# Differential attention with scores and maxima issued ahead of turns and combination, outputs one unit later

## What is computed

```python
def diff_attn_core(q, k, v, lam):
    s = jnp.einsum('bqhmd,bkhmd->bhmqk', q, k).astype(F32) * (B_HEAD_DIM ** -0.5)
    p = jax.nn.softmax(s, axis=-1)
    a = p[:, :, 0] - lam * p[:, :, 1]
    return jnp.einsum('bhqk,bkhd->bqhd', a.astype(v.dtype), v)
```

## Time and profile before

| | us |
|---|---|
| median of 3 runs | 1687.97 (1687.83 to 1690.42) |
| the profiled execution, its time | 1688.73 |
| the profiled execution, its span | 1687.0 |
| TensorE matmuls busy | 1563.1 (93% of the span) |
| VectorE busy | 905.6 (54%) |
| ScalarE busy | 520.5 (31%) |
| attention units, first scores to end of last O | about 313.8 to 428.1 |

### The profile page before, as it was taken

One profiled execution on the slowest core, in us unless ns is written; L12 is line 12 of the kernel. 1 busy time (PEld: TensorE's weight loads), 2 busy tenths in 40 slices (PEclk: granted clock), 3 DMA queues, 4 the chain that ended last, 5 costly groups with the idle time before them and its releaser, 6 DMA issues.

```text
span 1687.0 us, 22747 instructions
## 1 busy us (share of the span) xinstructions
PE 1563.1 (93%) x8480; PEld 1077.8 (64%) x8480; DVE 905.6 (54%) x1571; ACT 520.5 (31%) x836; POOL 156.2 (9%) x203
## 2 busy tenths in 40 slices
PE   5999999799899989999999989999999898898985
PEld 2788888577788868788788877785343333332441
DVE  2876526666558645576788788876212112121124
ACT  4422221567243354454432476322000000000011
POOL 2000010033110100001302130210000000000003
PEclk9999999789999999999999999999999999999998
DMA  9243352101332311223343202349999999999995
GB/s 383 113 160 140 113 216 109 57 14 31 113 138 104 119 53 51 100 88 151 142 149 129 101 26 77 132 189 371 405 423 423 423 422 423 423 422 423 422 383 214
DMA packets 57620, 353.08 MB, mean 209 GB/s; under 512 B 7376, under 2 KB 7632, under 8 KB 20544
## 3 DMA queue, kind: packets, MB, share of 16 engines
q1 hardware_dynamic: 43200, 307.41, 45.5%
q0 software_dynamic: 9248, 35.63, 5.7%
q10 hardware_dynamic: 5088, 8.92, 1.4%
HBM read 332.53 MB, written 23.59 MB: 211 GB/s over the span
## 4 chain that ended last, share of the span: by engine, by line
PE 64%; DMA 14%; DVE 9%; ACT 5%; SPq 4%; issue 4%; POOL 1%; ACTq 0%; DVEq 0%; POOLq 0%
PE ps L2266 11%; PE ps L2268 11%; PE ps L2267 11%; DMA early<-in_experts 10%; PE ps L2821 7%; PE ps L2307 4%; PE ps L2841 4%; SPq L705 3%; PE ps L2779 3%; PE ps L2484 3%; PE ps L2508 2%; DMA early<-in_ada 2%; PE ps L2218 1%; PE ps L2501 1%; ACT p L994 1%
## 5 line engine op out<-in xcount | busy, mean ns | idle before, releaser
L2266 PE MATMUL ps<-whi,xth 128*128 128x512 f32 (+1 forms) x768 | 300.8, 392 | 2.6 <-DVE xtl L1728 1.7
L2268 PE MATMUL ps<-whi,xtl 128*128 128x512 f32 (+1 forms) x768 | 297.0, 387 | 0.0
L2267 PE MATMUL ps<-wlo,xth 128*128 128x512 f32 (+1 forms) x768 | 296.7, 386 | 0.0
L2821 PE MATMUL ps<-early,xe_t 128*64 128x512 f32 x904 | 207.6, 598 | 31.0 <-DMA early<-in_experts 25.2
L2821 PEld LDWEIGHTS ps<-early,xe_t 128*64 128x64 f32 x904 | 60.9, 136 | 171.7 <-issue 104.5
L2266 PEld LDWEIGHTS ps<-whi,xth 128*128 128x128 f32 x768 | 145.2, 189 | 33.5 <-DVE xtl L1728 3.4
L2268 PEld LDWEIGHTS ps<-whi,xtl 128*128 128x128 f32 x768 | 145.0, 189 | 29.5
L2267 PEld LDWEIGHTS ps<-wlo,xth 128*128 128x128 f32 x768 | 145.3, 189 | 27.8
L2100 DVE TENSOR_TENSOR hid<-hid,ps 128x256 f32<-128x256 f32 x33 | 13.9, 421 | 251.3 <-ACT hid L1280 251.3
L1336 DVE TENSOR_TENSOR wlo<-raw,whi 128x2048 fp32r<-128x2048 f32 (+3 forms) x52 | 103.2, 1984 | 62.9 <-ACT whi L911 62.1
L1280 ACT ACTIVATE hid<-ps 128x256 f32<-128x256 f32 x33 | 12.7, 385 | 391.7 <-PE ps L2821 391.7
(11 more groups left out here) (463 smaller groups left out, 2712.1 us busy)
## 6 DMA issues: line engine op xcount, KB each, us to landing
early<-in_experts SPq DMA_DIRECT2D x128, 1024.0 KB, 26.4
raw<-in_experts SPq DMA_DIRECT2D x51, 1024.0 KB, 25.1
raw<-in_ada SPq DMA_DIRECT2D x40, 1024.0 KB, 6.7
ring<-in_experts SPq DMA_DIRECT2D x15, 1024.0 KB, 27.7
raw<-in_even SPq DMA_DIRECT2D x14, 1024.0 KB, 5.7
raw<-in_second SPq DMA_DIRECT2D x10, 1024.0 KB, 5.0
early<-in_ada SPq DMA_DIRECT2D x8, 1024.0 KB, 18.3
pair_dram<-tmp ACTq DMA_DIRECT2D x60, 128.0 KB, 6.9
```

The source lines that it names most:

```text
L2266: nc.tensor.matmul(v, a[0], b[0], start=first, stop=False)
L2267: nc.tensor.matmul(v, a[0], b[1], start=False, stop=False)
L2268: return nc.tensor.matmul(v, a[1], b[0], start=False, stop=last)
L2821: mm = nc.tensor.matmul(ps[SLOT * t:SLOT * t + SLOT, 4 + s, :], xe_t[:, 2 * i + k, SLOT * s:SLOT * s + SLOT], w[:, D * k + 512 * t:D * k + ...
```

## The change

Nothing is computed otherwise; three loops issue the same steps in another order, and the plan lists the jobs accordingly. TensorE's turn becomes scores(u+2), T(u), O(u-1); ScalarE's becomes exps(u+2), copy of T(u), copy of O(u-1); VectorE's becomes maxima(u+2), combine(u+1). The jobs keep their slots (scores 0 and 1, T 3, O 2), in the last two units too, where before they went on to slots of their own (O(22) to slot 0, T(23) to slot 1). The filler matmuls that were issued ahead of O(22) (`occupy_next`, L2246, two instructions) are gone.

```diff
--- before.py
+++ after.py
@@ -192,15 +192,18 @@
     ada(1, [4])
     for kt in range(4):
         plan.job("mix", "a", kt)
-    for u in range(2):
-        plan.job("S", "even", u, 0)
-        plan.job("S", "even", u, 1)
-    for u in range(E_UNITS):
-        plan.job("T", "even", u)
+    first = plan.next
+    for n in range(4):
+        plan.job("S", "even", n // 2, n % 2)
+    for u in range(E_UNITS + 1):
         if u + 2 < E_UNITS:
-            plan.job("S", "even", u + 2, 0)
-            plan.job("S", "even", u + 2, 1)
-        plan.job("O", "even", u)
+            for i in range(2):
+                plan.job("S", "even", u + 2, i, slot=(first + 1 + i) % SLOTS)
+        if u < E_UNITS:
+            plan.job("T", "even", u, slot=first)
+        if u:
+            plan.job("O", "even", u - 1, slot=(first + 3) % SLOTS)
+    plan.next = first
     chunk("eout", "o", 0, tiles)
     ada(1, [5])
     chunk("eout", "p", 1, tiles, ahead={m + 3: [("norm", "odd", m)] for m in range(3)})
@@ -1001,21 +1004,26 @@
             qk_high(2)
             exps(1)
             qk_high(3)
-            for u in range(E_UNITS):
-                v = filled(act, "T", "even", u)
-                if u >= 2:
-                    filled(act, "O", "even", u - 2)
-                n = keys(u // 4)
-                own(nc.scalar.activation(pt[:, u % 2, 0:n], v[:, 0:n], ACT.Copy), ev("T", "even", u))
-                if u == E_UNITS - 1:
-                    split_high(plan.through["eout", "p"] - 1)
-                if u + 2 < E_UNITS:
-                    exps(u + 2)
+            def kept(u):
                 v = filled(act, "O", "even", u)
                 o = o_rows[:, u // 4, P * (u % 4):P * (u % 4) + P]
                 own(nc.scalar.activation(o, v[:, 0:P], ACT.Copy, scale=soft[:, u % 4, 6:7]), ev("O", "even", u))
                 own.free(nc.scalar.activation(junk[:, P * (u % 4):P * (u % 4) + P], o, ACT.Square,
                                               accum_out=oss[:, u:u + 1]), s_oss)
+
+            for u in range(E_UNITS + 1):
+                if u + 2 < E_UNITS:
+                    exps(u + 2)
+                if u < E_UNITS:
+                    v = filled(act, "T", "even", u)
+                    if u >= 2:
+                        filled(act, "O", "even", u - 2)
+                    n = keys(u // 4)
+                    own(nc.scalar.activation(pt[:, u % 2, 0:n], v[:, 0:n], ACT.Copy), ev("T", "even", u))
+                if u:
+                    kept(u - 1)
+                if u == E_UNITS - 1:
+                    split_high(plan.through["eout", "p"] - 1)
             split_high(("eout", "p"))
             for kt in range(4, 8):
                 v = filled(act, "mix", "b", kt)
@@ -1534,10 +1542,10 @@
             maxima(1)
             qk_low(3)
             for u in range(E_UNITS):
+                if u + 2 < E_UNITS:
+                    maxima(u + 2)
                 if u + 1 < E_UNITS:
                     combine(u + 1)
-                if u + 2 < E_UNITS:
-                    maxima(u + 2)
             for h in range(2):
                 low_part(("eout", "p", h), 0, 1)
             for kt in range(4, 8):
@@ -2398,22 +2406,28 @@
 
             scores(0)
             scores(1)
-            for u in range(E_UNITS):
-                m, h = u // 4, u % 4
+            def weights_turned(u):
                 pe.wait_ge(s_comb, u + 1)
-                turn(("T", "even", u), [p0[:, u % 3, P * n:P * n + P] for n in range(keys(m) // P)],
-                     [P * n for n in range(keys(m) // P)])
-                if u + 2 < E_UNITS:
-                    scores(u + 2)
-                if u == E_UNITS - 2:
-                    occupy_next(2, "O", "even", u)
+                n = keys(u // 4) // P
+                turn(("T", "even", u), [p0[:, u % 3, P * k:P * k + P] for k in range(n)], [P * k for k in range(n)])
+
+            def unit_out(u):
+                h = u % 4
                 v = begin("O", "even", u)
                 evacuated(pe, "T", "even", u)
-                last = keys(m) // P - 1
+                last = keys(u // 4) // P - 1
                 for n in range(last + 1):
                     mm = nc.tensor.matmul(v[:, 0:P], pt[:, u % 2, P * n:P * n + P], vb[:, n, P * h:P * h + P],
                                           start=n == 0, stop=n == last)
                 end(mm, "O", "even", u)
+
+            for u in range(E_UNITS + 1):
+                if u + 2 < E_UNITS:
+                    scores(u + 2)
+                if u < E_UNITS:
+                    weights_turned(u)
+                if u:
+                    unit_out(u - 1)
             def norm(stage, m):
 
                 pe.wait_ge(s_xn2, SCALED[stage, m])
```

## The result

| | before | after |
|---|---|---|
| median, us | 1687.90 (1686.74 to 1690.42, 4 runs) | 1674.06 (1672.13 to 1676.55, 4 runs) |
| profiled execution: time, span | 1688.73, 1687.0 | 1673.72, 1671.9 |

The recorded ratio is 0.9911, with a 95% interval of 0.9896 to 0.9926. The two medians lie 13.8 us apart, a ratio of 0.9918, inside that interval. The forecast was 1677.9 us, and the range, which began at 1674.5, misses the median by 0.4 us. The sign was right and the size too small. A second timing gave 1674.96 us and 0.9920 (0.9907 to 0.9934), so the first was no accident.

A forecast was written before the change was run, and what follows sets the result against it. The prediction took a VectorE and ScalarE loop with the combination inside to bound the latent units; 0.88 + 1.06 + 2.1 + 6.05 = 10.1 us off the median 1687.97 gave 1677.9 us, range 1674.5 to 1682.5.

The forecast's parts named there:

- The loop, and what breaks it: Latent units: combination, first maximum and two exponentials hold a turn at 4.80 us; maxima ahead of the combination allow 4.25.
- Start of the loop (0.88): From the last split to scores(3): maxima of unit 2 no longer follow a combination and come 0.88 us earlier.
- Latent turns (6.05): Scores(12) to scores(23): eleven turns fall from 4.80 to TensorE's 4.25 us, 0.55 each, gain 6.05 us.
- Busy share: Rival, latent turns: TensorE's busy 4.49 us a unit is the floor; total gain 6.0 us, time 1682; chance 0.14.
- weight loads: Alternative bound, latent turns: loads busy 3.85 us a unit, 0.95 us to gain a turn, 10.4 over the stretch.
- Context units (1.06): Scores(3) to scores(8): TensorE's idle time, mostly 0.19 us ahead of each O, goes; gain 1.06 us.
- the first latent ones (2.1): Scores(8) to scores(12): idle time and a clock fall go, less some 0.8 us for a 3.6 us loop; gain 2.1.
- the clock rises earlier: Rival, context units: without waits the clock could rise there; gain about 13 us, time 1675; chance 0.11.
- step 3: Scores(8) to scores(12): counted idle time and a 1.4 us clock fall as removed; gain 2.1 us.
- The end (0): From scores(23) to the output product and GpSimd's last tile: about 0.1 us better, taken as 0.
- no-gain: Rival: a lengthened handover makes TensorE wait at scores(u+2); nothing gained, about 1687 us; chance 0.06.
- slower rival: Rival, latent units: the clock stays low, turns of 7.6 us; all sixteen low would give about 1730; chance 0.03.

The follow-up runs named there:

- the maxima alone: The kernel before with only VectorE's order changed, maxima(u+2) ahead of combine(u+1): 1711.05 us, ratio 1.0126 to the kernel before.
- the filler kernel: The kernel before with one extra 128x128 identity matmul ahead of each O of the eight context units: 1687.95 us, ratio 0.9998 to the kernel before.
- the last combination first: The changed kernel with VectorE taking combine(22) ahead of maxima(23), in that one turn: 1679.30 us, ratio 0.9938 to the kernel before.
- all but the maxima: The changed kernel with VectorE's old order, combine(u+1) ahead of maxima(u+2): 1689.95 us, ratio 1.0004 to the kernel before.

## Why the forecast was too low, step by step

**The loop, and what breaks it: right.** Maxima behind the combination did hold the turns. Without the new order on VectorE nothing is gained, and without the other engines' new order the same edit costs 21.7 us (1711.05 against 1689.33, the kernel before in the same session). O one unit later was needed too: in its own unit it waits 0.99 us a turn.

**Start of the loop (0.88): right.** Scores(3) start at 328.18, forecast 328.1, so 0.83 earlier; the stretch gained 1.13 because the first scores came 0.30 later.

**Latent turns (6.05): the term that failed.** The step is "the work alone is 4.80 - 0.38 - 0.17 = 4.25 us: scores 1.01 + 1.25". The 1.01 us from the first map's start to the second's was taken as work. Some 0.43 us of it were a wait. In the kernel before the exponential that empties the second slot runs from 387.12 to 388.02, and the second map starts at 388.16:

```profile
387.12 0.90 ACT L994 ACTIVATE p<-ps,stat 128x768 f32<-128x768 f32 x1
...
388.16 0.18 PEld L2266 LDWEIGHTS ps<-kt_h,qt_h 64*128 64x128 f32 x1
```

The view marks no wait there, because the first map's matmuls are counted busy meanwhile. The runs have the pair of maps at 2.67 us (kept in sequence), about 2.26 (before), 1.83 (slot free in time) and 1.25 (interleaved). With the slot free long before, as with the maxima alone (first map 388.99, second 389.57), the second still starts 0.58 us behind, so what the changed kernel has left is no wait of this kind. 4.25 - (2.26 - 1.83) = 3.82, and with T and O at 0.71 + 1.43 where I had 0.58 + 1.41, the turn is 3.97. Eleven turns then gain 8.68, where the term had 6.05. By itself this leaves the forecast at 1675.3, still inside the range; the range was missed because the clock, below, came on top.

Two of the eleven turns take 4.23 and 4.21 us (375.75 to 379.98, 391.87 to 396.08), and the trace shows why. In the turn before, VectorE's combination lies beside GpSimd's product and takes 1.73 us instead of 1.02. The maxima and exponentials follow later, and the second slot comes free at 376.43 (375.53 + 0.90), 0.68 us behind the first map's start; in the turn of 383.93 it was 0.44 behind (384.37):

```profile
371.57 1.04 POOL L779 TENSOR_TENSOR o_rows<-o_rows,stat 128x512 f32<-128x512 f32 x1
...
371.69 1.73 DVE L1535 SCALAR_TENSOR_TENSOR p<-p,stat,p 128x768 f32<-128x768 f32 x1
...
375.53 0.90 ACT L997 ACTIVATE p<-ps,stat 128x768 f32<-128x768 f32 x1
...
376.57 0.18 PEld L2274 LDWEIGHTS ps<-kt_h,qt_h 64*128 64x128 f32 x1
```

The second map starts 0.14 us behind that release, as it did in the kernel before, and 0.82 behind the first map instead of 0.58. It is the same wait that the 1.01 had hidden.

**Busy share and weight loads as bounds: both no bound.** The busy share put the floor at 4.49 and the kernel does 4.01 a turn (44.10 / 11). The busy row of the weight loads put it at 3.85, and in the changed kernel it is 39.05 / 11 = 3.55 for the same turns. No load became shorter: the single durations add up to 58.9 us in both kernels, and the busy row fell because loads of the two maps now lie side by side (x2 in the view) and count once. The Trainium skill (Perfetto Trace Analysis, Identifying the Most-Contended Engine) judges TensorE's headroom, among other things, by the sum of the loads' durations over the window, and not by matmul busy time. Here that sum is more than the stretch itself, 58.9 us in 52.78, so that it gives no floor. The busy row of the loads (3.85) came nearer to the 4.01 than that of the matmuls (4.49). The Trainium skill (TensorEngine Tiling, Key Properties) also says that different tiles of the array can load weights and multiply in parallel; the pair of maps at 1.25 us beside 1.23 for one map agrees. I did not use it; it would have warned me that 1.01 + 1.25 need not be a floor.

**Context units (1.06) and the first latent ones (2.1): the rival "the clock rises earlier" happened.** It had 0.11. The granted clock rose at about 333 instead of 348.3; the context turns then took 2.30 us (335.64, 337.94, 340.24) against the 2.2 that I gave for ScalarE's bound, and scores(8) to scores(9) took 3.52 instead of 4.80. I held its chance low because the clock had stayed low through all the context units before, with TensorE seldom idle. Which part of the new order raised it is open, as the filler kernel left it. The rival was sized at +3.2 us, and the two stretches gave 2.57 + 3.87 - 1.06 - 2.1 = 3.3 more than I had forecast. How much of that is the clock and how much the shorter pairs is not parted, so that the close match is in part luck.

The fall of the clock at 355 did not come in this trace, but it is not gone. In the second trace of the changed kernel the clock rose at 335.5 and fell from 356.0 to 359.4:

```profile
342.06:359.54 17.48, 15.57 (x89) 13.22 (x89) 14.02 (x21) 14.23 (x35) 8.13 (x9) 0.90 0.06 17
```

Scores(8) to scores(12) took 17.48 us there instead of 15.70, and the gain of the stretch was the 2.1 of the forecast. Of the traces with this order of issue in these units two have the fall (this one and the last combination first) and three have not, so step 3, which counted it as cured, was right in some executions only.

**The end (0): right in size.** -0.16. The output product starts 11.95 us behind scores(23), forecast 11.9. T(22) came 5.65 us behind scores(23), forecast 5.4, but it waited for VectorE's combination (1.61 us at 405.69) and not for slot 3, so that the near match of its start is in part luck. The stretch hides something more that I had not read: GpSimd's last tile, which sets the turns of `o_rows`, is itself 2.5 us longer than it need be.

**From stretches to the median.** The profile gained 15.0 us, the medians 13.8. Single executions of the kernel before lie 3.7 us apart, so that the 1.2 us between them is not explained further; a fall of the clock as above, 1.8 us, is one source of such differences. The two causes together, 2.6 us of floor and 3.3 us in the first stretches, would have made the forecast gain some 16 us. Neither the no-gain nor the slower rival showed.

Still open: how much of the clock's earlier rise is owed to each of the three reorderings, and what decides in which executions it falls again; no kernel parts these.

## What to carry to other kernels

Matmuls that use one half of the array's rows ran beside matmuls on the other half (two maps in 1.25 us, one in 1.23). So a time between two such starts is work only if the slot of the second was free: look up when its buffer was released before you add it to a floor. When an order on one engine is changed to break a loop, look at what the other engines' orders make of it in the same step; a piece alone cost more here (1.3%) than the whole brought (0.9%). A clock that rises sooner was worth time in the reordered kernel and nothing measurable where other engines held the turns, and one trace does not tell how often it rises or falls: read a second one of the same kernel.

## What was not expected of the hardware

- **Two engines in each other's way.** L1534 on VectorE works on one element a partition and takes 0.22 us (387.54). At 347.39 it took 0.95 and ended at 348.34, where GpSimd's L775 ended too (347.05 + 1.28 = 348.33). The other way round, GpSimd's L740 (0.19 us alone) took 1.52 from 413.74 to 415.26, beside VectorE's L1344, which ended at 415.20; L779 (1.04 alone) took 2.23 beside the next one. The one that comes second ends with the other or a little later, by no more than its own time alone, as if it had waited and not merely run slower. Not every pair does this: VectorE's two maxima from 385.35 took 1.95 us beside GpSimd's L742 at 386.57, as they do without it. The Trainium skill (SBUF — State Buffer, SBUF: two separate sides) describes a port pair that one of the two holds for a whole instruction while the other blocks, for VectorE instructions with two inputs in SBUF among others; these rows agree.
- **Two maps for the price of one.** Six passes on one half of the rows take 1.23 us, and twelve, six on each half, 1.25 us if they alternate. Issued map by map with nothing in the way they take 1.83. TensorE then does not keep to its list: all six passes of the first map stand ahead of the second map's, yet the second map's first pass starts at 384.51 and the first map's last at 384.97.
- **The clock of a TensorE shown busy.** With 0.19 us of waiting in front of each context O the granted clock stayed at 1.2 GHz until 348.3; with one more matmul in each of these places, and no other difference, it rose to 2.4 GHz at about 338. But a busy row alone does not bring it: with all but the maxima TensorE was busy 18.00 of 18.00 us from 330 to 348, and the clock stayed at 1.2 GHz until 348.3.
